# Hybrid encoder step with 32 experts on one core: output transfers issued inside attention, modulation rows fetched ahead of the expert weights, smaller bias transfers

## What is computed

```
mod = silu(c) @ w_ada + b_ada                        # 6 rows of 1024 for each group
sh1, sc1, g1, sh2, sc2, g2 = split(mod, 6)
mix, state = mixer(x * (1 + sc1) + sh1)              # w_in, attention A and B, convolution, w_out
x = layer_norm(ALPHA * x + g1 * mix, ln_g[0], ln_b[0])
ffn = moe_ffn(x * (1 + sc2) + sh2)                   # top 4 of 32 experts, each 12 MB of weights
x = layer_norm(ALPHA * x + g2 * ffn, ln_g[1], ln_b[1])
```

## Time and profile before

| | us |
|---|---|
| median of 3 runs | 1267.29 (1265.98 to 1271.55) |
| the profiled execution, its own time | 1268.6 |
| its span, first to last instruction | 1266.9 |
| TensorE busy | 1027.2 (81%) |
| VectorE busy | 314.9 (25%) |
| ScalarE busy | 181.1 (14%) |
| moved by DMA | 454.99 MB, 359 GB/s on average |
| the chain that ended last | PE 41%, DMA 24%, SP's queue 22%, DVE 6% |

### The profile page before, as it was taken

One profiled execution on the slowest core, in us unless ns is written; L12 is line 12 of the kernel. 1 busy time (PEld: TensorE's weight loads), 2 busy tenths in 40 slices (PEclk: granted clock), 3 DMA queues, 4 the chain that ended last, 5 costly groups with the idle time before them and its releaser, 6 DMA issues.

```text
span 1266.9 us, 30779 instructions
## 1 busy us (share of the span) xinstructions
PE 1027.2 (81%) x12329; PEld 484.9 (38%) x12330; DVE 314.9 (25%) x1021; ACT 181.1 (14%) x521; POOL 64.4 (5%) x142
## 2 busy tenths in 40 slices
PE   2789799798988778769788968997887897877973
PEld 1456554443443324224333424442433343332421
DVE  0286446611113112111211211121121121111215
ACT  0101333511111101011111101110110110110100
POOL 1820000000024000000000000000000000000000
PEclk9899899699998889989899989998898999888986
DMA  9997682879999999997998998099989989999994
GB/s 323 334 309 276 191 311 103 332 312 421 420 420 421 420 421 421 420 421 313 423 420 334 424 419 347 0 397 420 379 366 419 409 346 421 421 420 421 421 420 153
DMA packets 78409, 454.99 MB, mean 359 GB/s; under 512 B 9020, under 2 KB 17126, under 8 KB 29106
## 3 DMA queue, kind: packets, MB, share of 16 engines
q1 hardware_dynamic: 74092, 449.26, 87.5%
q10 hardware_dynamic: 4229, 4.41, 1.2%
HBM read 451.59 MB, written 2.61 MB: 359 GB/s over the span
## 4 chain that ended last, share of the span: by engine, by line
PE 41%; DMA 24%; SPq 22%; DVE 6%; issue 4%; ACT 1%; ACTq 1%; DVEq 0%
DMA w<-in_w_e_out 23%; PE bank L1766 15%; SPq L406 9%; PE bank L1795 8%; SPq L409 8%; PE bank L1746 3%; SPq L387 2%; PE comb L1729 2%; PE bank L1633 1%; PE comb L1633 1%; SPq L373 1%; PE bank L1783 1%; PE bank L1759 1%; DMA w<-in_w_ada 1%; DVE mt L1281 1%
## 5 line engine op out<-in xcount | busy, mean ns | idle before, releaser
L1766 PE MATMUL bank<-w,mt 128*32 128x512 f32 x3264 | 395.5, 628 | 51.9 <-DMA w<-in_w_e_in 51.7
L1795 PE MATMUL bank<-w,mt 128*32 128x256 f32 x3264 | 195.8, 385 | 47.0 <-DMA w<-in_w_e_out 32.9
L1766 PEld LDWEIGHTS bank<-w,mt 128*32 128x32 f32 x3264 | 96.8, 113 | 310.1 <-issue 209.3
L1273 DVE TENSOR_SCALAR mt<-bank 128x256 f32<-128x256 f32 x51 | 21.6, 424 | 696.7 <-PE bank L1766 696.7
L1795 PEld LDWEIGHTS bank<-w,mt 128*32 128x32 f32 x3264 | 98.3, 110 | 128.1 <-DMA w<-in_w_e_out 49.1
L1746 PE MATMUL bank<-pick,hb 128*128 128x32 bf16 x2448 | 79.2, 179 | 53.3 <-issue 53.0
L1746 PEld LDWEIGHTS bank<-pick,hb 128*128 128x128 bf16 x2448 | 74.9, 97 | 76.4 <-issue 76.0
L860 ACT ACTIVATE mt<-mt 128x256 f32<-128x256 f32 x51 | 21.3, 417 | 504.2 <-DVE mt L1273 504.2
L1729 PE MATMUL comb<-mt,gpickT 32*128 32x256 f32 x816 | 81.1, 471 | 0.5 <-ACT mt L869 0.5
L1747 PE MATMUL bank<-pick,hb 96*128 96x32 bf16 x408 | 72.4, 178 | 0.0
L1729 PEld LDWEIGHTS comb<-mt,gpickT 32*128 32x128 f32 x816 | 35.5, 204 | 51.3 <-issue 48.2
(11 more groups left out here) (339 smaller groups left out, 814.7 us busy)
## 6 DMA issues: line engine op xcount, KB each, us to landing
w<-in_w_e_in SPq DMA_DIRECT2D x256, 1024.0 KB, 26.2
w<-in_w_e_out SPq DMA_DIRECT2D x128, 1024.0 KB, 21.5
w<-in_w_ada SPq DMA_DIRECT2D x12, 2048.0 KB, 11.3
w<-in_w_in SPq DMA_DIRECT2D x3, 2048.0 KB, 22.5
w<-in_w_in SPq DMA_DIRECT2D x2, 1024.0 KB, 20.9
w<-in_w_out SPq DMA_DIRECT2D x4, 512.0 KB, 10.2
w<-in_w_out SPq DMA_DIRECT2D x2, 1024.0 KB, 12.7
w<-mod_rows SPq DMA_DIRECT2D x4, 512.0 KB
```

Source lines behind the costliest of these rows:

```text
L1766: ins = mm(quarter(bank[0][SLOTS * q:SLOTS * (q + 1), :], 0), xT[:, SLOTS * k:SLOTS * (k + 1)], quarter(slot[s], q), start=False, stop=(k ...
L1795: ins = mm(bank[0][SLOTS * q:SLOTS * (q + 1), 0:256], hid, slot[s][:, D * (k % 2) + 256 * q:D * (k % 2) + 256 * (q + 1)], start=False, sto ...
```

## The change

Five edits:

1. ScalarE's ten output transfers leave the place ahead of attention. The two of the convolution state are issued behind `exps(2)` in step 0, two of values in steps 1 and 2 each, two of keys in steps 3 and 4 each. An activation `Exp` of one element is put behind the last `store_mod`.
2. SP no longer issues four chunks of expert 0 ahead of the modulation rows; all eight come behind them.
3. `b_ada`: for each pair, four transfers of 2 rows each instead of one of 128. Rows 2 to 31 of each quarter are no longer written by a transfer, so VectorE zeroes `bada` at the start; SP and `add_mod` wait for that (`bada_zero`).
4. Piece 3 of `w_ada` comes in two transfers of 1 MB on two semaphores; TensorE waits for the second in the middle of `ada(3)`.
5. The four copies to `modc` become two.

```diff
-        ld_ada = [sem(f"ld_ada{s}") for s in range(4)]
+        ld_ada = [sem(f"ld_ada{s}") for s in range(5)]
...
+                if u == 3:
+                    for h in range(2):
+                        sp.dma_start(ring[:, 3, 2 * h:2 * h + 2], w_ada[0, 512 + 256 * h:768 + 256 * h, D:2 * D]
+                                     .rearrange("(k p) n -> p k n", p=P)).then_inc(ld_ada[(3, 4)[h]], 16)
+                else:
...
                 if half == 0:
+                    sp.wait_ge(bada_zero, 1)
                     if pair >= 2:
                         sp.wait_ge(mod_ready, pair - 1)
-                    src = bass.AP(tensor=b_ada.tensor, offset=b_ada.offset + D * pair, ap=[[256, 4], [0, 32], [1, 256]])
-                    sp.dma_start(bada[:, pair % 2, :], src).then_inc(ld_bada[pair % 2], 16)
+                    for q in range(4):
+                        at = D * pair + 256 * q
+                        sp.dma_start(bada[32 * q:32 * q + 2, pair % 2, :], b_ada[0:1, at:at + 256].to_broadcast([2, 256]))\
+                          .then_inc(ld_bada[pair % 2], 16)
...
             sp.wait_ge(proj_done, NPROJ)
-            load(0, 0, 0, 4)
             sp.wait_ge(ust_sent, 32)
...
-            load(0, 0, 4, 8)
+            load(0, 0, 0, 8)
...
             store_mod(5, 3)
+            a.activation(warm[0:1, 0:1], warm[0:1, 1:2], ACT.Exp)
             eng.wait_ge(proj_used, NPROJ)
...
-            dma_out(o_av_p[0, 0].rearrange("(t p) h d -> p t (h d)", p=P), vtok[:, 0:2, 0:256])
...
-            for dst, g in ((o_conv_p, 0), (o_conv_s, 1)):
-                eng.dma_start(dst[0, 0], ust[:, g, :]).then_inc(ust_sent, 16)
...
                 if s + 2 < NATT:
                     exps(s + 2)
+                if s == 0:
+                    send_conv()
+                elif s in (1, 2):
+                    send_values(s)
+                elif s in (3, 4):
+                    send_keys(s - 2)
...
+            v.memset(bada[:, :, :], 0.0).then_inc(bada_zero, 1)
...
             for g in range(2):
-                for h in range(2):
-                    ins = v.tensor_copy(modc[:, :, g, :].rearrange("p a (q h) -> p a h q", h=2)[:, :, h, :], pv[:, :, h, :, g])
-                    if (g, h) != (1, 1):
-                        link(ins)
+                ins = v.tensor_copy(modc[:, :, g, :].rearrange("p a (q h) -> p a h q", h=2), pv[:, :, :, :, g])
...
+                    if u == 3 and q == 2:
+                        pe.wait_ge(ld_ada[4], 16)
```

More of the change, by code:

```diff
@@ L227, in hybrid_streaming_encoder_step @@
             sem(n) for n in ("warm_done", "csig_done", "csil_done", "cT_done", "scT_done"))
+        bada_zero = sem("bada_zero")
         small_done, small_used, tabs_ready = sem("small_done"), sem("small_used"), sem("tabs_ready")
@@ L372, in ada_unit @@
                     sp.wait_ge(ada_done, u - (3 if u < 6 else 1))
-                sp.dma_start(ring[:, ada_slot(u)], w_ada[0, 512 * half:512 * (half + 1), D * pair:D * (pair + 1)]
-                             .rearrange("(k p) n -> p k n", p=P)).then_inc(ld_ada[ada_slot(u)], 16)
+                if u == 3:
[3 more added lines that the diff above has]
+                else:
+                    sp.dma_start(ring[:, ada_slot(u)], w_ada[0, 512 * half:512 * (half + 1), D * pair:D * (pair + 1)]
+                                 .rearrange("(k p) n -> p k n", p=P)).then_inc(ld_ada[ada_slot(u)], 16)
                 if half == 0:
+                    sp.wait_ge(bada_zero, 1)
                     if pair >= 2:
                         sp.wait_ge(mod_ready, pair - 1)
-                    src = bass.AP(tensor=b_ada.tensor, offset=b_ada.offset + D * pair, ap=[[256, 4], [0, 32], [1, 256]])
-                    sp.dma_start(bada[:, pair % 2, :], src).then_inc(ld_bada[pair % 2], 16)
+                    for q in range(4):
+                        at = D * pair + 256 * q
+                        sp.dma_start(bada[32 * q:32 * q + 2, pair % 2, :], b_ada[0:1, at:at + 256].to_broadcast([2, 256]))\
+                          .then_inc(ld_bada[pair % 2], 16)
             for u in range(4):
@@ L700, in dma_out, with send_conv, send_values, send_keys @@
                 eng.dma_start(dst, src).then_inc(st_out, 16)
-            dma_out(o_av_p[0, 0].rearrange("(t p) h d -> p t (h d)", p=P), vtok[:, 0:2, 0:256])
[L703 to L711, removed]
-            for dst, g in ((o_conv_p, 0), (o_conv_s, 1)):
-                eng.dma_start(dst[0, 0], ust[:, g, :]).then_inc(ust_sent, 16)
+            def send_conv():
+                eng.wait_ge(ust_ready, 1)
+                for dst, g in ((o_conv_p, 0), (o_conv_s, 1)):
+                    eng.dma_start(dst[0, 0], ust[:, g, :]).then_inc(ust_sent, 16)
+            def send_values(t):
+                if t < 2:
+                    dma_out(o_av_p[0, 0].rearrange("(t p) h d -> p t (h d)", p=P), vtok[:, 0:2, 0:256])
+                    dma_out(o_bv_p[0, 0].rearrange("p h d -> p (h d)"), vtok[:, 1, 256:384])
+                else:
+                    dma_out(o_av_s[0, 0, PAST - DEC:PAST].rearrange("p h d -> p (h d)"), vtok[0:32, 2, 0:256])
+                    dma_out(o_bv_s[0, 0, BCACHE - DEC:BCACHE].rearrange("p h d -> p (h d)"), vtok[0:32, 2, 256:384])
+            def send_keys(t):
+                eng.wait_ge(kt_ready, 3)
+                if t < 2:
+                    dma_out(o_ak_p[0, 0].rearrange("(t p) h d -> p t (h d)", p=P), ktok[:, 0:2, 0:256])
+                    dma_out(o_bk_p[0, 0].rearrange("p h d -> p (h d)"), ktok[:, 1, 256:384])
+                else:
+                    dma_out(o_ak_s[0, 0, PAST - DEC:PAST].rearrange("p h d -> p (h d)"), ktok[0:32, 2, 0:256])
+                    dma_out(o_bk_s[0, 0, BCACHE - DEC:BCACHE].rearrange("p h d -> p (h d)"), ktok[0:32, 2, 256:384])
             def exps(s):
@@ L925, in add_mod @@
                 dve.wait_ge(ada_done, 2 * pair + 2)
-                dve.wait_ge(ld_bada[pair % 2], 16 * (pair // 2 + 1))
+                dve.wait_ge(ld_bada[pair % 2], 64 * (pair // 2 + 1))
+                dve.wait_ge(bada_zero, 1)
                 if pair >= 4:
```

## The result

The changed kernel takes **1255.06 us** (median of 4 runs, 1253.84 to 1256.61) beside 1267.42 of the kernel before on the same chip; the ratio is 0.9892, 95% interval 0.9876 to 0.9909. The profiled execution took 1256.61 us (span 1254.6, before 1266.9). All 16 runs together have a median of 1256.8 us (1253.84 to 1262.62), the 88 runs of the kernel before in the later sets 1268.9 (1263.39 to 1273.48): 12.1 us, which taken from 1267.29 would lie inside the range. The two traces differ by 12.3 us, and this is the size I explain.

The account below looks back on a forecast made before the run. Experts bound by the weight stream and TensorE in turn, the head shifting both; 4.1 us before and in `ada(4)` plus 5.3 in attention, 9.4 off 1268.6, gave 1259.2, forecast as a median of 1257.9 us, range 1254.5 to 1262.5.

Parts of the forecast that it names:

- What bounds the kernel, and that the head reaches the end: Expert stage: bound by weight stream and TensorE in turn; bringing TensorE's arrival near 260 us forward brings the end forward.
- The rival in which the shift is lost there: Stream held at 260 us by something with its own time, so the head's gain is lost; 1267.3 us, chance 0.05.
- Bias rows, 2.7 us: SP's queue ahead of `w_ada` piece 4: two `b_ada` transfers on four engines delay it; 2.7 us, bounds 0.7 and 6.3.
- the rival that they are not in the way: SP's queue slow for itself, or small transfers cost what they relieve; only attention's 5.3 us remain, 1262.0 us, chance 0.10.
- `ada(4)` at the full clock, 1.4 us: TensorE at `ada(4)`: shorter idleness keeps the clock at 2.4 GHz, 1.93 instead of 3.33 us; bounds 0 and 1.4.
- Pieces and copies, 0 on the path: `ada(3)` and `modc`: any gain ends in TensorE's idle time before `ada(4)`, as long as piece 4 lands last; 0.
- 24 small issues at no cost: SP's queue: 24 small bias transfers instead of 6 are covered by pieces in flight and waits; 0, else 1.6 us.
- Outputs: Start of attention: moving ten output issues starts transposes 3.5 us earlier, VectorE's third maximum then limiting; whole place 5.3 us.
- The other 1.8 us: Attention's first steps: ScalarE bounds them at 2.3 to 2.4 instead of 2.83 us, four steps saving 0.45 each.
- The rival of a clock that falls in one place: Clock still falls at `ada(4)` or in attention's first steps, 1.4 or 1.8 us less gain; 1259.5 us, chance 0.20.
- Edit 2, 0: Modulation rows ahead of expert 0's chunks: rows needed only in step 11, weights at 236 us; value 0, cost 0.
- The slower rival: Attention: moved issues held in ScalarE's queue by transfers in flight, delaying copies TensorE waits for; 1282.5 us, chance 0.03.

Follow-up runs that it names:

- ln_rows: The changed kernel with `ln_g` and `ln_b` of the first layer norm each as four transfers of 2 rows instead of one of 128; 1254.51 us.
- spread_all: The changed kernel with `ln_g`, `ln_b` in four 2-row transfers each, `x_sample` in four of 32 rows and `conv_w` in two; 1250.86 us.
- bias_alone: The kernel before with only the `b_ada` change, four transfers of 2 rows for each pair; 1264.30 us, ratio 0.9977.
- bias_twice: The kernel before with the first two bias transfers each made twice; 1275.14 us, ratio 1.004.
- bias_later_old: The kernel before with small bias transfers only for pairs 0 and 1, later pairs still one transfer of 128 rows; 1265.25 us, ratio 0.9975.
- after: The changed kernel itself in its first set of runs, with the first profiled execution; 1255.06 us, ratio 0.9892.
- after_again: The changed kernel run again later, an expert's two block ends read with stated bounds instead of a plain register load; 1257.07 us, ratio 0.9906.
- sends_later: The changed kernel with values and keys issued in attention's steps 6 to 9 instead of 1 to 4; 1255.95 us, ratio 0.9891.
- x_rows: The changed kernel with `x_sample` in four transfers of 32 rows and `conv_w` in two; 1253.91 us, ratio 0.9884.
- after_m: The changed kernel with an expert's two block ends read with stated bounds instead of a plain register load; 1258.84 us, ratio 0.9937.
- pieces_alone: The kernel before with only piece 3 of `w_ada` in two transfers and two copies to `modc`; 1269.82 us, ratio 1.0005.
- bias_spread: The kernel before with each bias transfer of 128 rows cut into four of 32 rows that all 16 engines can share; 1264.85 us, ratio 0.9975.

## Why the prediction was right or wrong

- **What bounds the kernel, and that the head reaches the end: right.** The experts begin 12.5 us earlier, the stream resumes 12.9 earlier, and the end is 12.3 earlier. The rival in which the shift is lost there falls. One sign of being wrong did come, a shift at 260 larger than that of the end, by 0.6 us. It says little at this size: over all traces of this section the shifts of the experts' start and of the end agree within 1.6 us either way (15.3 and 15.3 in `ln_rows`, 20.5 and 21.1 in `spread_all`).
- **Bias rows, 2.7 us: the step that failed.** The place and the reason were right, and the rival that they are not in the way falls with `bias_alone`. The size was 5.2 us (5.3 by the means). Two things were missing. The two transfers ahead of piece 4 gave 3.6 to 4.0 us, not 2.7: I priced only the rows on four engines at the pure row rate (1.35 a transfer), and 1.5 (`bias_twice`) to 1.8 us (`bias_later_old`, 3.6 for two; 1.9 to 2.0 by the means) were measured. And I counted two transfers where the trace has three: the one right behind piece 4, whose rows move while piece 4's own are under way, is worth 0.9 to 2.0 us (1.3 by the means). How much of this reaches the end is less sure: alone, edit 3 took 4.0 us by the medians and 2.9 by the ratio, no more than the forecast's 4.1 for this place with `ada(4)`. The place of the hole was read wrongly too: `ln_b` is issued from 56.30 to 59.45, and the share falls behind that (0.54, 0.33, 0.76 in 58 to 64), not in it. My upper bound of 6.3 did hold the value; but I put the range's low end at "the far bound of the bias rows" and then wrote 1254.5, which is 3.4 us below the forecast where 6.3 - 2.7 = 3.6 belongs, and took nothing for the other place's upper bound (6.5 against 5.3). Both together reach 1253.1, which holds the time. That this set fell outside the range and the later ones inside is partly chance.
- **`ada(4)` at the full clock, 1.4 us: right** in this trace (1.93 us). It is not certain: they took 1.93 or 1.94 us in `after`, `after_again`, `bias_alone` and `spread_all`, after 1.47 to 2.36 us of idleness, and 2.53 to 3.24 in `sends_later`, `x_rows`, `after_m` and `ln_rows`, after 2.37 to 3.72. So this term was a matter of luck in the first trace.
- **Pieces and copies, 0 on the path: right**, shown by the time of `pieces_alone`. The wait for piece 3 is gone, as said, and the projection waits for `w_in` instead (2.06 us). That `tabs` would be up to 3 us later was wrong: it came 0.7 us later (31.30), the transposes of `x` 3.2 us later. The delayed transfer in ScalarE's queue was `x_sample`, which has the same four-run pattern and which I had not looked at. What it costs was hidden by the wait for `tabs` behind it, and `x_rows` shows what it was worth, together with `conv_w`.
- **24 small issues at no cost: right on the path.** The second four took 7.22 us of SP's queue from 4.05 on, behind pieces in flight, and SP was still ahead of where it had been (`w_in` from 14.56 instead of 19.80).
- **Outputs: right to the first step, 3.5 us forecast and 3.6 measured**, with the third maximum as the next limit. (TensorE's gap is 5.3 - 3.5 = 1.8 us by my own sum, not the 1.6 that I wrote; it measured 1.70.) **The other 1.8 us were 2.1, by another way.** I expected ScalarE to bound the steps at 2.3 to 2.4 us at the full clock. The issues bound none: activations run beside them. Steps take 1.6 to 1.7 or 2.24 us at 1.00, and 2.8 at 0.50, and TensorE has no idle time in the first five of the six: my premise that its part is under 2 us fails for the steps with the larger logits. In this trace the clock was 0.52 from 140.0 to 146.8, half as long as before (147 to 160); in `after_m`, where it did not fall, the same steps gave 5.0 us. The rival of a clock that falls in one place had the right event and too small a price: 1.8 us, where the two traces differ by 2.9.
- **Edit 2, 0: not tried alone.** SP waited 14.5 us for the convolution outputs instead of 18.5.
- **The slower rival** needed 1.6 us an issue. The longest is 1.17, above the 0.8 that I had named as a sign; it held one copy by 0.3 us and lengthened no step.

## What to carry to other kernels

Look for transfers whose outermost dimension is small (here four runs, repeated or not) in a queue that the critical path shares, and count also the ones issued right **behind** the transfer that is waited for. Price them by an experiment that adds one and one that removes one, since the row rate gave 1.35 us where 1.5 to 2.0 were measured. Read the issue time in the queue and the landing apart, as they had different causes here. When one such pattern is found, search for all of its kind: three more places (`ln_g`, `ln_b`, `x_sample`, the last with `conv_w`) gave another 6 us. And ask for each engine's clock at each place before adding up a step: one place here was worth 2.1 or 5.0 us by whether the clock fell.

## What the runs showed that I had not expected

- Twelve transfers of 2 KB in place of three of 128 KB (pairs 0 to 2) were 5.3 us better at piece 4; part of that is the rows left out, but the same bytes as twelve transfers of 32 KB (`bias_spread`) were 2.5 better too. The Trainium skill, DMA: Bandwidth & Descriptors, Rules for kernel authors, advises to coalesce many small transfers into a large one, since under 64 KB one pays mostly overhead. That did not hold here. By the same section's rule on the outermost dimension the large form was confined to four engines, and the trace of `bias_spread` agrees (piece 4 issued at 60.94 instead of 64.28). The measurement decides.
- ScalarE's activations run beside a transfer's issue in its queue: two ran inside one of 1.17 us, and the next began only at its end.
- The same program's granted clock falls in different places from execution to execution (in attention's first steps for 6.8 us in the first trace of the change, for 3.4 in `after_again`, not at all in `after_m`). The times of one program spread over some 10 us, and the first four runs lay 1.7 us below the median of all 16.
